# Channel-major products of a decoder trunk: the 128 weights of a stationary operand four elements apart in SBUF

## The reference, cut to what matters

```python
def conv_ffn(h, w_up, conv_w, conv_b, w_down):
    u = h @ w_up                                   # (256, 1024) @ (1024, 5632)
    ...                                            # causal depthwise convolution of width 3 along the tokens
    gate, val = jnp.split(c, 2, axis=-1)
    return (jax.nn.gelu(gate, approximate=True) * val) @ w_down

def odd_mixer(h, w_in, w_out):
    qkv = (h @ w_in).reshape(B, S, 3, SB_HEADS, HEAD_DIM)   # (256, 1024) @ (1024, 3072)
    return stick_breaking_attention(qkv[:, :, 0], qkv[:, :, 1], qkv[:, :, 2]) @ w_out
```

## Time and profile before

| what | value |
|---|---|
| median of 3 runs | 655.75 us |
| the profiled execution's own time | 656.09 us |
| its span in the trace | 654.3 us |
| PE busy (matmul) | 646.6 us, 99% |
| PEld busy (weight loads) | 539.7 us, 82% |
| DVE / ACT / POOL busy | 459.7 / 385.3 / 161.6 us |

### The profile page before, as it was taken

One profiled execution on the slowest core, in us unless ns is written; L12 is line 12 of the kernel. 1 busy time (PEld: TensorE's weight loads), 2 busy tenths in 40 slices (PEclk: granted clock), 3 DMA queues, 4 the chain that ended last, 5 costly groups with the idle time before them and its releaser, 6 DMA issues.

```text
span 654.3 us, 9977 instructions
## 1 busy us (share of the span) xinstructions
PE 646.6 (99%) x3574; PEld 539.7 (82%) x3574; DVE 459.7 (70%) x627; ACT 385.3 (59%) x561; POOL 161.6 (25%) x123
## 2 busy tenths in 40 slices
PE   9999999999999999999999999999999999999996
PEld 6888887667888989888888888877889888888885
DVE  6498766887697878785457646576688787886532
ACT  7646445775766767576335527565567576767330
POOL 0321310001044443441001001580123434343000
PEclk9999999999999999999999999999999999999999
DMA  8987633005356364547652666204255554544601
GB/s 352 338 300 272 238 129 129 1 2 193 128 200 240 138 237 147 219 166 260 234 194 85 256 218 229 69 2 188 102 188 197 188 197 168 216 156 174 247 1 65
DMA packets 18971, 115.60 MB, mean 177 GB/s; under 512 B 2911, under 2 KB 3453, under 8 KB 6013
## 3 DMA queue, kind: packets, MB, share of 16 engines
q1 hardware_dynamic: 17789, 111.52, 45.9%
q10 hardware_dynamic: 1152, 3.67, 1.6%
HBM read 114.14 MB, written 1.05 MB: 176 GB/s over the span
## 4 chain that ended last, share of the span: by engine, by line
PE 97%; DVE 1%; issue 1%; ACT 0%; POOL 0%; DVEq 0%; POOLq 0%
PE ps L1429 27%; PE ps L1437 14%; PE ps L1386 12%; PE ps L1388 12%; PE ps L1387 12%; PE ps L1466 5%; PE ps L1521 2%; PE ps L1765 1%; PE ps L1915 1%; PE ps L1649 1%; PE ps L1899 1%; PE ps L1377 1%; PE ps L1693 1%; PE ps L1928 1%; PE ps L1615 1%
## 5 line engine op out<-in xcount | busy, mean ns | idle before, releaser
L778 DVE TENSOR_TENSOR wlo<-raw,whi 128x2048 fp32r<-128x2048 f32 x99 | 226.5, 2319 | 71.5 <-ACT whi L413 71.4
L413 ACT CAST whi<-raw 128x2048 fp32r<-128x2048 f32 x99 | 185.8, 1917 | 48.6 <-PE ps L1388 42.6
L1429 PE MATMUL ps<-xpair,whi 128*128 128x512 f32 x768 | 179.4, 390 | 0.0
L1429 PEld LDWEIGHTS ps<-xpair,whi 128*128 128x128 f32 x768 | 142.5, 188 | 28.7
L1334 POOL TENSOR_TENSOR hidf<-act_g,conv 128x512 f32<-128x512 f32 x22 | 76.0, 3452 | 85.0 <-ACT act_g L671 85.0
L1437 PEld LDWEIGHTS ps<-xpair,wlo 128*128 128x128 f32 x768 | 95.4, 192 | 1.9
L1437 PE MATMUL ps<-xpair,wlo 128*128 128x256 f32 x768 | 96.1, 283 | 0.0
L1386 PE MATMUL ps<-whi,hid_hi 128*128 128x512 f32 x176 | 68.5, 389 | 0.0
L1387 PE MATMUL ps<-wlo,hid_hi 128*128 128x512 f32 x176 | 68.5, 389 | 0.0
L1388 PE MATMUL ps<-whi,hid_lo 128*128 128x512 f32 x176 | 68.5, 389 | 0.0
L1386 PE MATMUL ps<-whi,xpair 128*128 128x512 f32 x168 | 67.6, 402 | 0.0
(11 more groups left out here) (197 smaller groups left out, 786.8 us busy)
## 6 DMA issues: line engine op xcount, KB each, us to landing
raw<-in_weights SPq DMA_DIRECT2D x101, 1024.0 KB, 4.9
c_gpost<-in_gpost ACTq DMA_DIRECT2D x4, 512.0 KB, 4.8
raw<-in_weights SPq DMA_DIRECT2D x3, 512.0 KB, 6.6
c_gpre<-in_gpre ACTq DMA_DIRECT2D x3, 512.0 KB, 4.1
h<-in_x SPq DMA_DIRECT2D x2, 512.0 KB, 3.8
out<-h SPq DMA_DIRECT2D x4, 256.0 KB, 2.0
raw<-in_weights SPq DMA_DIRECT2D x2, 256.0 KB, 4.7
t<-in_masks SPq DMA_DIRECT2D x1, 512.0 KB, 12.0
```

Of the source, the lines that this page charges most:

```text
L413: act.copy(whi[:, slot, :], raw[:, slot, :]).then_inc(hi_done, 1)
L778: dve.tensor_tensor(wlo[:, slot, :], raw[:, slot, :], whi[:, slot, :].bitcast(F32), ALU.subtract).then_inc(lo_done, 1)
L1429: ins = pe.matmul(ps[:, b0 + m, :], whi[:, slot, cols], xpair[:, kt].rearrange("p a c -> p (a c)"), start=kt == 0, stop=kt == KT - 1, skip ...
```

## The change

The stationary operand of both channel-major products takes every fourth element of a block of 512, beginning at `m`, in place of 128 neighbours. The host permutes the columns of each such block so that column `4 j + m` of the block holds what was column `128 m + j`. Each matmul multiplies the same numbers as before and writes them to the same place. The blocks that are used token-major (chunk 0 of either up-projection, the v columns of the odd layer) keep their order. Units, transfers, splits, waits and the order of instructions are as before.

```diff
@@ channel_high
-                    cols = slice(b * BLK + m * P, b * BLK + (m + 1) * P)
+                    cols = slice(b * BLK + m, (b + 1) * BLK, BLK // P)
                     ins = pe.matmul(ps[:, b0 + m, :], whi[:, slot, cols], xpair[:, kt].rearrange("p a c -> p (a c)"),
                                     start=kt == 0, stop=kt == KT - 1, skip_group_check=True)
@@ lay_out (host)
-    w_in1 = np.concatenate([v[:, :BLK], q[:, :BLK], k[:, :BLK], q[:, BLK:], k[:, BLK:], v[:, BLK:]], axis=1)
+
+    def tiles_mixed(w):
+
+        return w.reshape(D, -1, BLK // P, P).transpose(0, 1, 3, 2).reshape(D, -1)
+
+    w_in1 = np.concatenate([v[:, :BLK]] + [tiles_mixed(w) for w in (q[:, :BLK], k[:, :BLK], q[:, BLK:], k[:, BLK:])] +
+                           [v[:, BLK:]], axis=1)
 
     def up(layer):
 
         v = ffn_w_up[layer].reshape(D, 2, UP_CHUNKS, 2 * P).transpose(0, 2, 1, 3).reshape(D, 2 * D_FF)
-        return blocks_in(v)
+        return blocks_in(np.concatenate([v[:, :BLK], tiles_mixed(v[:, BLK:])], axis=1))
```

## The result

The changed kernel takes 748.95 us (median of 4 runs, 748.87 to 749.02) against 655.83 us before (4 runs, 655.68 to 656.0): a ratio of 1.142, interval 1.1406 to 1.1435. The profiled execution took 748.87 us, 92.8 us more than the 656.09 us of before. The forecast was 740.5 us.

What follows compares the result with a forecast made beforehand. PE, busy 99% of the span, was taken to bound the kernel. Low products' 70.4 us and high products' 14.3 us, together 84.7 us, on 656.09 us gave 740.8 us profiled, 740.5 us as median; range 720 to 770 us (chance 0.58).

Steps and rivals of the forecast that it cites:

- The bound and the point: PE's rate is the time; low products (L1437) have 12.8 ns before the load sets their cadence, high ones (L1429) 120.6.
- What costs nothing: Host permutation, transfers, result banks, instruction order and waits stay as before, so nothing there adds time.
- The low term: L1437: a load of 211.4 ns sets the cadence in place of 119.7, 91.7 ns x 768 = 70.4 us.
- DVE's 0.82 ns per far element: Extra per element, L984 reading SBUF 32 bytes apart against contiguous L1056; gives a load 104.5 ns more.
- The bound of 160.5 ns: L1429 and L1437 loads, if reading and filling the array overlap: 31.3 + 14.3 = 45.6 us, 701 us in all.
- The high term: L1429: load stays hidden, but its wider span costs the stream 18.6 ns per matmul, x 768 = 14.3 us.
- the 6 ns that the residue unit had: Its loads 8 bytes apart cost the matmul stream 6.2 ns, taken as the price per 512 bytes spanned.
- The span alone: Both products lose 18.6 ns, loads keep their rate: 28.6 us, 684 us; chance 0.21 together with an overlapped load.
- no change: The array's fill sets the load's 106.9 ns and reading has room, so 656 us; chance 0.06.
- faster: The changed kernel gets faster by more than the 0.2% that a measurement can tell; chance 0.10.
- the far slower case: L1429 and L1437: far element costs 1.9 ns, load and stream add up: low 109 us, high 26 us, 791 us; chance 0.05.

Runs made afterwards that it cites:

- near_32: Kernel before the change (loads of neighbours), but low products (L1437) move 32 columns in place of 256; 668.72 us, ratio 1.0195.
- step 2: Changed kernel with both products loading elements two apart (8 bytes) in place of four, host layout matched; 661.25 us, ratio 1.0084.
- step 3: Changed kernel with both products loading elements three apart (12 bytes) in place of four, columns not laid out for it; 704.73 us, ratio 1.0747.
- far_32: Changed kernel (loads four elements apart), but low products (L1437) move 32 columns in place of 256; 794.14 us, ratio 1.2107.
- H L H L: Each high matmul followed by its low one: kernel before 657.69 us; with only low loads four elements apart 659.87 us, only high loads 745.64 us.

## Why the prediction was right

- **The bound and the point.** PE is the time, and the low products had little to spare before the load sets their cadence: 12.8 ns as forecast, 119.7 - 108.8 = 10.9 ns by `near_32`. That held: at step 2 the low cadence stays at 120.0 ns, at step 3 it leaves (174.4). That loads are pipelined L1437 shows: 192 ns from start to end at a cadence of 119.7 ns. That the 106.9 ns of L1797 are the load's rate was my reading of one run of 16; L1693 and the two runs with 32 columns bear it out.
- **What costs nothing.** Host, transfers, splits, DVE and ACT stood still to within 0.4 us of busy time.
- **The low term**, 91.7 ns forecast, 110.0 measured (84.5 us for 70.4). DVE's 0.82 ns per far element came out some 11% under the load's own 0.92 ns, which is 13.6 of the 18.3 ns missed; the rest is 2.8 ns from the stream beside it and 1.9 ns from taking 106.9 ns for the near load, where these loops show 108.8. That so close a price came from another engine and another distance (32 bytes) is in part luck: PE's own moving side pays 0.46 ns. What the prediction had right by its reasoning is that a far load costs on top of the near one and sets the low cadence. The bound of 160.5 ns, reading and filling overlapped (31.3 us, 768 x 40.8 ns above the 119.7), is excluded by the 226.9 ns of `far_32`.
- **The high term**, 18.6 ns forecast, 11.3 measured (8.7 us for 14.3). This step failed: I drew a straight line through 256, 512 and 1024 bytes. The table shows a jump at step 2, of the 6 ns that the residue unit had, and a slope of about a third of it afterwards.
- The two errors have opposite signs, 14.1 us under and 5.6 us over, and leave 8.5 us. Part of the nearness of the total is thus luck too, but not that it lay within 720 to 770 us: with the high term right and the low one as forecast it would have been 735 us, with the low one right and the high one as forecast 755 us.
- **Rivals.** The span alone (684 us) falls with the low cadence of 229.7 ns, and so does no change; faster, whose chance of 0.10 was my estimate alone, falls with the two columns, which nowhere shrink; the far slower case (791 us) with 229.7 and 238.8 ns in place of its 243 + 18.6 = 262 ns for either kind, 26 us on the high side. The loads pay 118.1 ns at 16 bytes (226.9 against the 108.8 ns of neighbours); at 8 bytes the runs only show that the load takes no more than 120.0 ns.

Left open: why the high cadence rises by 6.9 ns at a step of 8 bytes while the low one doesn't. Nor is it shown where the 11.3 ns of the high term go in the order H L H L: far loads beside the long stream add nothing to the pair there (353 against 354 ns), but the pair of near loads already stands 6 ns above the 347 ns of the two kinds in runs.

## What to carry to other kernels

Look at a load's cadence, not its duration, and hold it against the stream of the matmul just ahead: by far the most of what it costs is the excess over that one (beside the 256 columns 226.9 - 119.7 = 107.2 of the 110.0 ns; beside the 512 columns, whose 227.5 ns are no shorter than the load's 226.9, it still cost 11.3 ns). Keep at least two of a stationary float32 operand's elements in each 16 bytes (low cadence 120.0 ns with elements 8 bytes apart, 174.4 at 12, 229.7 at 16), and the moving operand's elements side by side (227.5 ns against 451.3 at 8 bytes). Where a far load can't be avoided, order the matmuls so that it follows a long stream: the same loads cost 85 us or, beside the long stream, 2 us here, each against the kernel of its own order with near loads.

## What the runs showed of the hardware beyond that

- A moving float32 (fp32r) operand read 8 bytes apart costs nearly as much as at 16 bytes, 451 against 461 ns for 512 columns (227.5 side by side), while loads at 8 bytes leave the low cadence at 120.0 ns (119.7 side by side) and add 6.9 ns to the high one.
- Moving 32 columns in place of 256 behind each load made the kernel slower, 668.7 for 655.9 us with near loads, since TensorE's granted clock fell (mean 0.965 over the run; with far loads 0.896) and the high products that followed paid for it: 32 of them took 7.38 us at a clock of 1.00 and 8.98 us at 0.81. The loads kept about their pace: in `far_32` 12 in 2.46 us at 0.53, 22 in 4.79 us at 1.00.
- A far element costs a load 0.92 ns more on 0.85 (108.8 / 128) and the moving stream 0.46 ns more on 0.44 (227.5 / 512): either about doubles, so the price isn't one fixed time per element. DVE's 0.82 ns on 1.08 compares two different lines at 32 bytes; no run tested it by itself.
